# The last group of the second MLP product in another product order, with the late tokens' output finished two products ahead

## The reference

```python
def rms_norm(x, gain):
    xf = x.astype(jnp.float32)
    y = xf * lax.rsqrt(jnp.mean(xf * xf, axis=-1, keepdims=True) + EPS)
    return (y * gain.astype(jnp.float32)).astype(x.dtype)
...
        x = x + g2[:, None, :] * squared_relu_mlp(h, w_ff1[layer], w_ff2[layer])
...
    return rms_norm(x, final_gain)
```

## Time and profile before

| what | us |
|---|---|
| three timed runs | 2471.39, 2474.40, 2474.52; median 2474.4 |
| span of the profiled execution | 2470.8 |
| TensorE busy | 2396.2 (97%) |
| VectorE busy | 1909.1 (77%) |
| ScalarE busy | 1019.1 (41%) |
| GpSimd busy | 376.7 (15%) |

### The profile page before, as it was taken

The page is one execution under the profiler, slowest core; times in us unless marked ns, Lnnn a source line. Parts: engine busy times, 40 slices in busy tenths (PEclk is TensorE's granted clock), DMA queues, the critical chain, the costliest instruction groups (busy, mean ns, idle before and its releaser), DMA issues.

```text
span 2470.8 us, 36978 instructions
## 1 busy us (share of the span) xinstructions
PE 2396.2 (97%) x14009; PEld 2090.3 (85%) x14009; DVE 1909.1 (77%) x2246; ACT 1019.1 (41%) x1346; POOL 376.7 (15%) x154
## 2 busy tenths in 40 slices
PE   5999999999999999999999999999999999999997
PEld 3689988888888887887899999999997888888885
DVE  4346557777778457765998988898888989889988
ACT  4244322222223223223656655656554343344433
POOL 0100143333333443443300000000000000000000
PEclk9999999999999999999999999999999999999998
DMA  9945553333333565565455656565569888998883
GB/s 360 365 140 167 179 171 119 104 118 102 110 102 111 179 208 201 198 202 209 154 188 208 231 195 222 207 220 203 214 261 344 319 321 294 365 350 281 316 309 131
DMA packets 184073, 536.07 MB, mean 217 GB/s; under 512 B 13312, under 2 KB 13584, under 8 KB 176784
## 3 DMA queue, kind: packets, MB, share of 16 engines
q1 hardware_dynamic: 183520, 533.88, 60.7%
q10 hardware_dynamic: 432, 0.54, 0.1%
HBM read 467.26 MB, written 67.12 MB: 216 GB/s over the span
## 4 chain that ended last, share of the span: by engine, by line
PE 60%; issue 21%; POOL 8%; DVE 7%; DMA 2%; ACT 1%; SPq 0%; POOLq 0%; DVEq 0%; ACTq 0%
POOL w_lo L578 8%; PE banks L2260 8%; PE banks L2262 7%; PE banks L2261 7%; PE banks L2218 6%; PE banks L2220 6%; PE banks L2219 6%; PE banks L1827 3%; PE banks L1829 3%; PE banks L1828 3%; DVE w_lo L1507 2%; DMA raw<-in_w_stream 2%; PE banks L1811 1%; PE banks L1812 1%; PE banks L1813 1%
## 5 line engine op out<-in xcount | busy, mean ns | idle before, releaser
L902 ACT ACTIVATE w_hi<-raw 128x1024 fp32r<-128x1024 f32 x434 | 457.4, 1059 | 575.5 <-PE banks L2262 277.1
L1507 DVE TENSOR_TENSOR w_lo<-raw,w_hi 128x1024 fp32r<-128x1024 f32 x434 | 523.2, 1219 | 77.1 <-ACT w_hi L902 76.9
L612 ACT ACTIVATE w_hi<-raw 128x1024 fp32r<-128x1024 f32 x184 | 194.9, 1059 | 723.2 <-PE banks L1813 480.0
L578 POOL TENSOR_TENSOR w_lo<-raw,w_hi 128x1024 fp32r<-128x1024 f32 x144 | 357.9, 2486 | 805.5 <-ACT w_hi L612 805.5
L2260 PE MATMUL banks<-w_hi,hid 128*128 128x512 f32 x896 | 348.9, 389 | 4.5 <-DVE y L1547 2.2
L2262 PE MATMUL banks<-w_hi,hid 128*128 128x512 f32 x896 | 348.6, 389 | 0.0
L2261 PE MATMUL banks<-w_lo,hid 128*128 128x512 f32 x896 | 348.6, 389 | 0.0
L1811 PE MATMUL banks<-h_hi,w_hi 128*128 128x512 f32 x720 | 289.1, 402 | 0.0
L1165 DVE SCALAR_TENSOR_TENSOR ada_acc<-ada_w,cs,ada_acc 128x512 f32<-128x512 f32 x195 | 222.5, 1141 | 84.1 <-DMA ada_w<-in_w_ada 77.3
L1813 PE MATMUL banks<-h_hi,w_lo 128*128 128x512 f32 x720 | 281.0, 390 | 0.0
L1812 PE MATMUL banks<-h_lo,w_hi 128*128 128x512 f32 x720 | 280.6, 390 | 0.0
(11 more groups left out here) (302 smaller groups left out, 4505.2 us busy)
## 6 DMA issues: line engine op xcount, KB each, us to landing
raw<-in_w_stream SPq DMA_DIRECT2D x440, 512.0 KB, 4.7
hid<-hid_kept SPq DMA_DIRECT2D x111, 1024.0 KB, 6.6
ada_w<-in_w_ada SPq DMA_DIRECT2D x176, 512.0 KB, 4.8
hid_kept<-half SPq DMA_DIRECT2D x32, 1792.0 KB, 6.8
ada_w<-in_w_ada SPq DMA_DIRECT2D x32, 256.0 KB, 5.3
x_tok<-in_x SPq DMA_DIRECT2D x4, 1024.0 KB, 10.6
x_res<-in_x SPq DMA_DIRECT2D x4, 1024.0 KB, 7.4
x_kept<-x_res SPq DMA_DIRECT2D x4, 1024.0 KB, 6.9
```

The costliest lines, as they stand in the source:

```text
L578: pool.tensor_tensor(w_lo[:, r % 2], raw[:, r], w_hi[:, r % 2].bitcast(F32), ALU.subtract).then_inc(lo_done, 1)
L902: act.activation(operand_w(par, i)[0], raw_of(o), ACT.Copy).then_inc(hi_done, 1)
L1507: dve.tensor_tensor(lo, raw_of(OPERAND[i // 2] + i % 2), hi.bitcast(F32), ALU.subtract).then_inc(lo2_done, 1)
```

## The change

In the last of the 16 groups the products are taken in the order 0 2 3 4 5 1 6. The weight sums are made in another order to suit it (T4 now goes into the place of B12), and the last group is written out by functions of its own on TensorE, ScalarE and VectorE. Quarters are complete in the order (1, 1), (1, 0), (0, 0), (0, 1): both quarters of the late tokens come first, after product 5, which two more products follow. VectorE sums, scales and thereby frees the late tiles before it adds product 1. The last residual addition is cut into its two token tiles, and each tile is stored in two column halves (two runs of 512 columns each, 512 KB a store), the one as soon as ScalarE has scaled it, the other after VectorE.

```diff
+LAST_ORDER = (0, 2, 3, 4, 5, 1, 6)
+LAST_OPERAND = (B11, B11, B12, B11, B12, B21, B22)
+LAST_FINAL = ((1, 1), (1, 0), (0, 0), (0, 1))
...
                 sp.wait_ge(norm_act, i + 1)
+                sp.dma_start(column_half(out[t * P:(t + 1) * P, :], 0), column_half(y[:, t], 0)).then_inc(stored, 16)
                 sp.wait_ge(norm_dve, i + 1)
-                sp.dma_start(out[t * P:(t + 1) * P, :], y[:, t]).then_inc(stored, 16)
-            sp.wait_ge(stored, 16 * TT)
+                sp.dma_start(column_half(out[t * P:(t + 1) * P, :], 1), column_half(y[:, t], 1)).then_inc(stored, 16)
+            sp.wait_ge(stored, 16 * 2 * TT)
...
+            def last_hi(i):
+
+                g = F1_GROUPS + F2_GROUPS - 1
+                act.wait_ge(unit_used, 14 * g + (U_RING + i - 3))
+                o = LAST_OPERAND[i // 2] + i % 2
+                if i in (0, 1, 10, 11, 12, 13):
+                    landed, count = landed_of(o, g)
+                    act.wait_ge(landed, count)
+                else:
+                    act.wait_ge(sum_made, 8 * g + {2: 2, 3: 4, 4: 1, 5: 3, 6: 7, 7: 8, 8: 5, 9: 6}[i])
+                act.activation(operand_w(0, i)[0], raw_of(o), ACT.Copy).then_inc(hi_done, 1)
...
+                if k < 7:
+                    act.wait_ge(x_made, k + 1)
                 if k:
                     act.wait_ge(last_squared, 2 * k)
                 for t in (2 * i, 2 * i + 1):
+                    if k == 7:
+                        act.wait_ge(x_made, k + 1 + t % 2)
...
-            for k in range(4, 7):
-                last_squares(k, 1)
+            last_squares(4, 1)
+            last_squares(5, 1)
             last_sqrt(1)
             last_row(1, 2)
+            last_row(1, 3)
+            last_squares(6, 1)
             last_squares(7, 1)
             last_sqrt(0)
-            last_row(1, 3)
             last_row(0, 0)
             last_row(0, 1)
...
+                if to_last:
+                    sum_t3(g + 1, 1)
+                    last_low(2)
...
+            def last_t4(h):
+
+                g = F1_GROUPS + F2_GROUPS - 1
+                dve.wait_ge(sum_made, 8 * g + (2 + 2 * h))
+                dve.wait_ge(lo2_done, 14 * g + (5 + h))
+                landed, count = landed_of(B21 + h, g)
+                dve.wait_ge(landed, count)
+                dve.tensor_tensor(raw_of(B12 + h), raw_of(B21 + h), raw_of(B11 + h), ALU.subtract).then_inc(sum_made, 1)
...
+            def last_add(p):
+
+                g, at = F1_GROUPS + F2_GROUPS - 1, LAST_ORDER.index(p)
+                i, j = TARGET[p]
+                dst = tile_pair(y, 1, i, j)
+                dve.wait_ge(unit_used, 14 * g + (U_RING + 2 * at + 2))
+                dve.wait_ge(y_added, 7 * (F2_GROUPS - 1) + at)
+                dve.tensor_tensor(dst, chain_banks(0, p)[:], dst, ALU.add).then_inc(y_added, 1)
+
+            def last_group():
+
+                sum_t2(F1_GROUPS + F2_GROUPS - 1, 1)
+                last_low(3)
+                last_low(4)
+                last_t4(0)
+                last_add(0)
+                last_low(5)
+                last_t4(1)
+                last_t1(0)
+                last_low(6)
+                last_t1(1)
+                last_add(2)
+                last_low(7)
+                last_low(8)
+                last_add(3)
+                last_low(9)
+                last_low(10)
+                last_add(4)
+                final_gate(4)
+                last_low(11)
+                final_add(4)
+                last_low(12)
+                last_add(5)
+                final_gate(5)
+                final_add(5)
+                last_low(13)
+                last_sum(1)
+                last_reciprocal(1)
+                last_row(1, 2)
+                last_row(1, 3)
+                last_add(1)
+                final_gate(6)
+                final_add(6)
+                last_add(6)
+                final_gate(7)
+                final_add_by_tile(7)
+                last_sum(0)
+                last_reciprocal(0)
+                last_row(0, 0)
+                last_row(0, 1)
...
+            def final_add_by_tile(k):
+
+                yp, xp, row = final_parts(k)
+                dve.wait_ge(gated, k + 1)
+                for t in range(2):
+                    dve.tensor_tensor(xp[:, t], xp[:, t], yp[:, t], ALU.add).then_inc(x_made, 1)
...
-            group_dve(F1_GROUPS + F2_GROUPS - 1, 0, 1, False, False, None, 4)
-            last_sum(1)
-            final_gate(7)
-            last_reciprocal(1)
-            final_add(7)
-            last_row(1, 2)
-            last_sum(0)
-            last_row(1, 3)
-            last_reciprocal(0)
-            last_row(0, 0)
-            last_row(0, 1)
+                group_dve(g + F1_GROUPS, (g + 1) % 2, 1, g == BLOCKS, True, None, g - 9 if g - 9 in range(4) else None, to_last=g == F2_GROUPS - 2)
+            last_group()
...
+            def last_group_pe():
+
+                g, added = F1_GROUPS + F2_GROUPS - 1, 7 * (F2_GROUPS - 1)
+                for i in range(14):
+                    p, h = LAST_ORDER[i // 2], i % 2
+                    banks = two_banks[{"x": 2, "y": 3, "z": 0}[CHAIN[p]]]
+                    pe.wait_ge(lo2_done, 14 * g + (i + 1))
+                    if h == 0:
+                        pe.wait_ge(hid_landed[p], 16 * (F2_GROUPS - 1) + 16)
+                        pe.wait_ge(y_added, added + {0: -7, 2: 1, 3: -1, 4: 2, 5: 3, 1: -5, 6: 4}[p])
+                    wh, wl = operand_w(0, i)
+                    for k in range(2):
+                        ws_, start = slice(k * 512, (k + 1) * 512), p in (0, 1, 3) and h == 0 and k == 0
+                        for t in range(2):
+                            xh, xl = (hid_r[:, p, 2 * h + k, a, t * P:(t + 1) * P] for a in range(2))
+                            dst = banks[:, t]
+                            pe.matmul(dst, xh, wh[:, ws_], start=start, stop=False, skip_group_check=True)
+                            pe.matmul(dst, xh, wl[:, ws_], start=False, stop=False, skip_group_check=True)
+                            mm = pe.matmul(dst, xl, wh[:, ws_], start=False, stop=(h == 1 and k == 1), skip_group_check=True)
+                    mm.then_inc(unit_used, 1)
...
-            with pe.Fori(1, BLOCKS) as k:
+            with pe.Fori(1, BLOCKS - 1) as k:
                 group_pe(2 * k + F1_GROUPS, 1)
                 group_pe(2 * k + (F1_GROUPS + 1), 0)
+            group_pe(F1_GROUPS + F2_GROUPS - 2, 1)
+            last_group_pe()
```

More of the change, by code:

```diff
@@ L1020, in _ @@
                 for i in range(14):
-                    operand_hi(g + F1_GROUPS, (g + 1) % 2, i)
+                    if g < F2_GROUPS - 1:
+                        operand_hi(g + F1_GROUPS, (g + 1) % 2, i)
+                    else:
+                        last_hi(i)
                 if g - 9 in range(4):
                     last_squares(g - 9, 0)
-            for k in range(4, 7):
-                last_squares(k, 1)
+            last_squares(4, 1)
+            last_squares(5, 1)
             last_sqrt(1)
             last_row(1, 2)
+            last_row(1, 3)
+            last_squares(6, 1)
             last_squares(7, 1)
             last_sqrt(0)
-            last_row(1, 3)
             last_row(0, 0)
@@ L1610, in f1_dve, with group_dve @@
                 sum_t3(g + 1, 1)
-            def group_dve(g, par, n, first=False, after=True, late=None, scaled=None):
+            def group_dve(g, par, n, first=False, after=True, late=None, scaled=None, to_last=False):
                 operand_low(g, par, 3)
@@ L1641, in group_dve @@
                 operand_low(g, par, 13)
-                if after:
-                    if scaled is not None:
-                        final_scale(scaled)
-                    operand_low(g + 1, 1 - par, 0)
-                else:
-                    final_gate(5)
-                    final_add(5)
-                add_y(g, par, n, 5, first)
-                if after:
-                    operand_low(g + 1, 1 - par, 1)
-                    sum_t3(g + 1, 0)
-                    sum_t2(g + 1, 0)
+                if scaled is not None:
+                    final_scale(scaled)
@@ L1654, in group_dve @@
+                operand_low(g + 1, 1 - par, 0)
+                add_y(g, par, n, 5, first)
+                operand_low(g + 1, 1 - par, 1)
+                sum_t3(g + 1, 0)
+                sum_t2(g + 1, 0)
+                if to_last:
+                    sum_t3(g + 1, 1)
+                    last_low(2)
+                else:
                     operand_low(g + 1, 1 - par, 2)
                     sum_t3(g + 1, 1)
-                else:
-                    final_gate(6)
-                    final_add(6)
@@ L1659, in group_dve, with last_low @@
                 add_y(g, par, n, 6, first)
+            def last_low(i):
+                g = F1_GROUPS + F2_GROUPS - 1
+                dve.wait_ge(hi_done, 14 * g + (U_RING + i + 1))
+                hi, lo = operand_w(0, i)
```

(14 more changed lines are left out.)

10 lines of the change are left out of this document (4 added, 6 removed).

## The result

The changed kernel takes 2482.8 us (median of six runs, 2481.8 to 2491.5), the kernel before beside it 2472.7 (six runs, 2470.8 to 2474.5). By the medians it is 10.1 us slower, where I had forecast 4.5 and a range that ended at 2481.5. The ratio is 1.0051, 95% interval 1.0041 to 1.0060; the medians alone give the lower end of it. Two later measurements of the same kernel gave 1.0049 (1.0035 to 1.0062) and 1.0041 (1.0028 to 1.0054), with medians 12.4 and 9.9 us apart. The execution that was profiled took 2482.64 us, its span is 2480.8 (10.0 more than before); what lies around the span is 1.8 us. The 3.6 us that I carried from before compared a profiled span with the median of other executions.

What follows compares the result with a forecast made beforehand. The prediction took TensorE as the bound, every wait of it paid in full. Wait +4.6, clock +2.0 and tail -2.1 summed to +4.5 us on 2474.4, so 2478.9 us, range 2475.5 to 2481.5.

Steps and rivals of the forecast that it cites:

- idle time between products 0 and 2: Last group: TensorE waits 4.6 us for VectorE to read product 0 out of the banks that product 2 needs.
- clock behind it: After TensorE's idle stretch: clock falls, costing 2.0 us, within bounds 1.46 and 2.75, or 0 if spared.
- tail: From TensorE's last matmul's end (E) to the span's end: 14.6 us instead of 16.66, a gain of 2.1.
- written-out TensorE code: Straight-line code replacing TensorE's last loop turn: costs nothing, since matmuls queued ahead hide its reading.
- T3(0) and T2(0) start at 2413.03 and 2414.30 as before: First sums in the VectorE list leading to product 0's addition: start unchanged, with no added wait.
- The walk through the list: VectorE's program order from T3(0) to product 0's addition, ending 2426.04; TensorE goes on at 2426.07, idle 4.6 us.
- late weights for T3(1): VectorE's list ahead of product 0's addition: longest landing, 8.2 us instead of 6.0, adds at most 0.5 us idle.
- my upper bound of 2.75: TensorE's restart: most the clock's fall would cost, from an earlier restart after 5.34 us idle.
- Rival 1: TensorE's restart at 2426: clock stays down long or weights land late; +5.25, +5.75 with late landing; chance 0.36.
- Rival 2: Behind TensorE's idle stretch: clock does not fall; +2.5 us, 2476.9; chance 0.11.
- Rival 3: Between products 0 and 2: VectorE reads product 0 in time, wait hidden; -2.1 us, 2472.3; chance 0.04.
- rival 4: Tail: half stores don't overlap, each paying in turn; 8.5 us more than the sum, 2487.4; chance 0.03.

Runs made afterwards that it cites:

- experiment 3: Kernel before, old order, with TensorE's last loop turn written out behind the loop: 2474.8 against 2472.3 us, ratio 1.0011.
- experiment 8: Kernel before with half stores, old order, and TensorE's last two groups written out: 2475.4 against 2472.6 us, ratio 1.0009.
- experiment 13: Kernel before with one turn of TensorE's loop written out, measured again beside the unaltered kernel: 2475.2 us, ratio 1.0010.
- experiment 10: Kernel before with three turns of TensorE's loop written out behind the loop: 2472.5 against 2472.2 us, ratio 1.0005.
- experiment 11: Kernel before with one turn of TensorE's loop written out ahead of the loop: 2474.7 against 2472.2 us, ratio 1.0011.
- the controls: On one chip: kernel before unaltered 2472.2 us, with one turn written out 2475.2; changed kernel with half stores 2482.6, with whole stores 2481.2.
- experiment 5: Changed kernel measured again, unaltered: 2485.0 us in five runs, ratio 1.0049.
- experiment 15: Changed kernel with each tile stored whole instead of in halves, measured again: 2481.2 us, ratio 1.0035.
- experiment 1: Changed kernel with product 0's addition moved ahead of low parts 3 and 4 and sum T4(0) in VectorE's list: 2476.5 us, ratio 1.0018.
- experiment 12: Kernel before, unaltered, timed like a changed one: 2472.2 us, ratio 1.0001.
- experiment 9: Changed kernel, order 0 3 2 5 4 1 6, product 3's addition earlier, VectorE's late scalings given to GpSimd and ScalarE: 2474.5 against 2472.2 us, ratio 1.0012.
- experiment 6: Changed kernel with each tile stored in one piece after both halves are made: 2480.1 us, ratio 1.0035.

## Why the prediction was wrong

| term of the sum | forecast | three traces of the changed kernel | mean |
|---|---|---|---|
| idle time between products 0 and 2 | +4.6 | 6.55, 5.57, 6.38 | +6.2 |
| clock behind it | +2.0 | 2.0, 3.0, 2.2 | +2.4 |
| tail | -2.1 | 15.21, 15.26, 15.27 us, against 16.66 | -1.4 |
| written-out TensorE code | 0 | no trace; medians of experiments 3, 8, 13 | +2.6 |
| sum | +4.5 | | +9.8 |

The three measured differences are 10.1, 12.4 and 9.9 us, so the terms leave 0.1 to 2.6 us, no more than the uncertainty of these medians. Three terms come from traces and the fourth from medians. In the profiled execution of the changed kernel the place of the fourth is taken by what the result section showed, a clock that fell at 1906 us and 1.0 us more of waiting ahead of the last group.

**The step that failed most is "the straight-line code that takes the place of TensorE's last loop turn I cost at nothing".** I had asked only for an idle stretch at the group's start, found cover for that in the first two groups, and took it for the whole cost. There is no such stretch, and yet the kernels with one turn written out were 2.4 to 2.8 us slower by their medians. What makes them slower is open (experiments 10, 11 and the controls); what is shown is that a kernel with that edit and nothing else was not free.

**The second is "T3(0) and T2(0) start at 2413.03 and 2414.30 as before"**, which priced the wait for the weights of T3(0) at nothing. Here the mechanism was right and the term too small. In five traces of the changed kernel, half or whole stores, the wait for the weights and TensorE's idle time are 1.74 and 6.55, 0.74 and 5.57, 1.56 and 6.38, 0.69 and 5.51, 0.97 and 5.79 us: the idle time is 4.82 us plus that wait, each time within 0.02. The walk through the list was thus right to 0.2 us. In the trace of before that wait was zero; two other traces of kernels with the loop show 0.27 and 0.57 us, and the fourteen with written-out code 0.35 to 2.35, mean 1.5. Whether the written-out code itself makes the weights later, three traces against fourteen don't settle. Such a wait is harmless while another product covers it and becomes TensorE's as soon as the list is the path. I had kept late weights for T3(1), at most 0.5 us, but not for T3(0), which stands first in the list.

**The clock** fell as forecast; how long it stays down does not follow the idle time: 6.55 us of it cost 2.0, 5.57 us cost 3.0, since the clock fell 2.7 us ahead of the restart in the one and 0.8 in the other. Experiments 5 and 15 lie above my upper bound of 2.75 (3.0 and 2.9); bounds from two restarts were too narrow.

**The tail**: product 6's addition (E + 1.44 for + 1.5) and the first late store (E + 8.0 for + 7.9) came as reckoned. The bytes did not: they began 1.2 us behind that issue, where I had taken 0.85 from whole stores, and from there to the end of the span it took 6.05 us for 5.85. From a stretch of loads I had allowed 0 to 0.2 for the smaller pieces; beside whole stores the halves cost 0.4, most of it in the late first bytes.

**The rivals.** Rival 1 took the right side, for a part of the right reason (weights late, clock long); its worked-out ceiling of +5.75 was short by the written-out code, by T3(0) and by the tail. Rival 2 (no fall of the clock) came true only where the idle time shrank to 1.4 us, in experiment 1. Rival 3 is refuted by the trace. So is rival 4: the four late stores began at 2473.59 and all bytes had moved by 2480.0, 6.4 us. Had each store paid in turn the fixed cost of about 2 us that the Trainium skill gives ("DMA: Bandwidth & Descriptors", section "Anatomy of one DMA — SWDGE (gpsimd) path", a fit for transfers that GpSimd issues), the estimate was 12.8; the trace, whose stores SyncE issues, does not bear out a sum in turn.

## What to carry to other kernels

When two producers that share a buffer are put side by side, walk the consumer's list up to the release, and add to it every wait that an earlier instruction of that list shows anywhere in the trace, not only at this place; then ask first whether the release can move ahead in the list (here three instructions moved behind one addition gave back 6 of 10 us). An end that is brought forward by reordering pays only as far as the engine that carries the reordered work has slack: here VectorE's list was full and kept the gain to 1.5 us, about what written-out kernels lost elsewhere, so that with all of TensorE's waits in the last group removed the new order was still only level with the old one. Measure what written-out code costs with a kernel that has that and nothing else.

## What the hardware showed that was not expected

- **The same idle time, two clocks.** About 1904 us every kernel here has an idle stretch of 2.1 to 2.2 us. In the trace of before the clock stays at 1.00 behind it. Windows of the kernel before, then of the same program measured again (experiment 12), where it falls to 0.50 and seven matmuls go into 2 us in place of eleven:

```profile
1906.00:1908.00 2.00, 2.00 (x11) 1.65 (x10) 2.00 (x3) 0.54 (x1) 0.00 (x0) 1.00 0.66 193
```

```profile
1906.00:1908.00 2.00, 2.00 (x7) 1.51 (x6) 2.00 (x3) 0.00 (x0) 0.00 (x0) 0.50 0.56 170
```

  It cost 1.7 us there, and it happened in nine of the seventeen traces. It is one source of the scatter of 2.5 us.
- **GpSimd stops VectorE whole.** The 3.28 us of experiment 9 fit what the Trainium skill says in "SBUF — State Buffer" (section "SBUF: two separate sides"): the two engines share a pair of ports that one holds for a whole instruction, when VectorE reads two tensors from SBUF and GpSimd reads SBUF too. The trace agrees: the residual addition, with two such inputs, waited for the end of GpSimd's instruction; product 1's addition, which reads one input from PSUM, took 1.22 us beside the first multiplication.
- **Kernels with one turn of TensorE's loop written out were slower, and no row shows where**: 2.4 to 2.8 us by the medians of four comparisons (three behind the loop, one ahead of it), nothing that can be told from 0 with three turns (1.0005), and none for the unaltered program (1.0001). The cause is open.
- **The first byte of a store of 2 KB pieces is late**: 1.2 us behind the issue for half stores, 0.8 for whole ones (experiment 6).
